# Latent attention in a two-layer block: maxima written negated, the rotation's last steps on GpSimd, and the former pair's sums and scaling ahead of the second head's last maxima

## The reference

```python
def mla_mixer(h, positions, w_in, q_g, kv_g, w_uq, w_ukv, w_out):
    """Non-causal multi-head latent attention with decoupled rotary key."""
    cq, ckv, kr = jnp.split(h @ w_in, [Q_LORA, Q_LORA + KV_LORA], axis=-1)
    q = (rms_norm_2(cq, q_g) @ w_uq).reshape(bsz, seq, C_HEADS, C_NOPE + C_ROPE)
    kv = (rms_norm_2(ckv, kv_g) @ w_ukv).reshape(bsz, seq, C_HEADS, C_NOPE + C_V)
    ...
    q_rope = apply_rope_2(q[..., C_NOPE:], cos, sin)
    k_rope = apply_rope_2(kr[:, :, None, :], cos, sin)
    ...
    def attend(qblk):
        s = jnp.einsum("bqhd,bkhd->bhqk", qblk, kf, preferred_element_type=jnp.float32) * scale
        pr = jax.nn.softmax(s, axis=-1)
        return jnp.einsum("bhqk,bkhd->bqhd", pr.astype(v.dtype), v)
    ...
    return o.reshape(bsz, seq, C_HEADS * C_V) @ w_out
```

## Time and profile before

| what | us |
|---|---|
| median of 3 runs | 1922.03 |
| the profiled execution, its own time | 1919.63 |
| its span, first to last instruction | 1917.8 |
| TensorE busy | 1860.2 (97%) |
| VectorE busy | 1153.8 (60%) |
| ScalarE busy | 736.8 (38%) |
| GpSimd busy | 166.2 (9%) |

### The profile page before, as it was taken

One profiled execution on the slowest core, in us unless ns is written; L12 is line 12 of the kernel. 1 busy time (PEld: TensorE's weight loads), 2 busy tenths in 40 slices (PEclk: granted clock), 3 DMA queues, 4 the chain that ended last, 5 costly groups with the idle time before them and its releaser, 6 DMA issues.

```text
span 1917.8 us, 24685 instructions
## 1 busy us (share of the span) xinstructions
PE 1860.2 (97%) x8914; PEld 1508.7 (79%) x8914; DVE 1153.8 (60%) x1645; ACT 736.8 (38%) x1074; POOL 166.2 (9%) x175
## 2 busy tenths in 40 slices
PE   7998999999999999999999999999999999999998
PEld 6786788888888877887788888888656688888887
DVE  7768644884674778777543434376788554334344
ACT  5355222542342444554432322334544342323231
POOL 0020000300000011010000000002366200000000
PEclk9998999999999999999999999999999999999999
DMA  5233003233333342311333333332110133333332
GB/s 211 88 121 99 1 3 122 64 99 99 98 89 99 99 121 77 94 60 45 93 99 97 92 96 98 99 98 78 56 34 23 45 88 99 99 98 92 95 99 88
DMA packets 47929, 165.68 MB, mean 86 GB/s; under 512 B 5217, under 2 KB 7265, under 8 KB 47713
## 3 DMA queue, kind: packets, MB, share of 16 engines
q1 hardware_dynamic: 46368, 161.27, 28.0%
q10 hardware_dynamic: 1472, 3.22, 0.5%
HBM read 162.38 MB, written 2.10 MB: 86 GB/s over the span
## 4 chain that ended last, share of the span: by engine, by line
PE 83%; DVE 10%; ACT 3%; issue 2%; POOL 1%; DMA 0%; DVEq 0%; ACTq 0%; POOLq 0%
PE ps L611 25%; PE ps L613 24%; PE ps L612 24%; PE ps L867 2%; PE ps L970 1%; DVE w_lo L2039 1%; POOL x L532 1%; PE ps L831 1%; DVE mla_mx L2634 1%; DVE tmp L2076 1%; ACT w_hi L1417 1%; PE ps L1216 1%; DVE qk_c L2753 0%; DVE mx L2556 0%; PE ps L800 0%
## 5 line engine op out<-in xcount | busy, mean ns | idle before, releaser
L1417 ACT ACTIVATE w_hi<-raw 128x1024 fp32r<-128x1024 f32 x281 | 297.7, 1060 | 792.1 <-PE ps L613 792.0
L611 PE MATMUL ps<-h_hi,w_hi 128*128 128x512 f32 (+1 forms) x1288 | 509.8, 396 | 10.9 <-DVE w_lo L2039 9.9
L612 PE MATMUL ps<-h_lo,w_hi 128*128 128x512 f32 (+1 forms) x1288 | 500.0, 388 | 0.0
L613 PE MATMUL ps<-h_hi,w_lo 128*128 128x512 f32 (+1 forms) x1288 | 499.9, 388 | 0.0
L2039 DVE TENSOR_TENSOR w_lo<-raw,w_hi 128x1024 fp32r<-128x1024 f32 x281 | 346.7, 1234 | 125.9 <-ACT w_hi L1417 124.4
L611 PEld LDWEIGHTS ps<-h_hi,w_hi 128*128 128x128 f32 x1288 | 243.3, 189 | 65.1 <-issue 13.0
L613 PEld LDWEIGHTS ps<-h_hi,w_lo 128*128 128x128 f32 x1288 | 243.0, 189 | 50.4
L612 PEld LDWEIGHTS ps<-h_lo,w_hi 128*128 128x128 f32 x1288 | 243.3, 189 | 49.9 <-issue 2.2
L611 PE MATMUL ps<-hid_hi,w_hi 128*128 128x512 f32 (+1 forms) x716 | 273.6, 382 | 1.7 <-DVE w_lo L2039 0.9
L613 PE MATMUL ps<-hid_hi,w_lo 128*128 128x512 f32 (+1 forms) x716 | 272.6, 381 | 0.0
L612 PE MATMUL ps<-hid_lo,w_hi 128*128 128x512 f32 (+1 forms) x716 | 272.6, 381 | 0.0
(11 more groups left out here) (404 smaller groups left out, 2524.2 us busy)
## 6 DMA issues: line engine op xcount, KB each, us to landing
raw<-in_panels SPq DMA_DIRECT2D x296, 512.0 KB, 3.6
x_in<-in_x SPq DMA_DIRECT2D x8, 256.0 KB, 5.7
x<-in_x ACTq DMA_DIRECT2D x1, 2048.0 KB, 8.4
out<-y SPq DMA_DIRECT2D x16, 128.0 KB, 1.8
first<-in_first SPq DMA_DIRECT2D x1, 1568.0 KB, 11.7
second<-in_second ACTq DMA_DIRECT2D x1, 512.0 KB, 3.5
small<-in_small ACTq DMA_DIRECT2D x1, 332.0 KB, 3.9
masks<-in_masks SPq DMA_DIRECT2D x1, 256.0 KB, 11.9
```

The costliest lines, as they stand in the source:

```text
L611: nc.tensor.matmul(out, a[0], b[0], start=start, stop=False)
L612: nc.tensor.matmul(out, a[0], b[1], start=False, stop=False)
L613: return nc.tensor.matmul(out, a[1], b[0], start=False, stop=stop)
L1417: nc.scalar.activation(w_high(panel, i), raw[:, panel % 4, :], ACT.Copy).then_inc(w_hi_ready, 1)
```

## The change

`mla_mx`, the instruction of line 2638 and its semaphore `negm_ready` are gone: the reduction writes the negated maximum straight into `mla_negm`, and `turn` waits for the fourth reduction. The bound by -1e20 is left out with it. `quad_finish` of the second, third and fourth group of four heads is issued by GpSimd, at the start of turns 2, 6 and 10, ahead of `pair_low` and `place_two`; the first group's stays on VectorE. In odd turns TensorE issues `totals(p - 1)` where `values(p, 0)` was, right behind scores 1, and `values(p, 0)` where `totals(p - 1)` was, behind scores 2 (in turn 1, where there are no totals, `values(0, 0)` moves too); VectorE does `shares` and `pair_result` ahead of largest 2 and 3 and `shift_of`, and no longer behind them.

```diff
+        def quad_finish(i):
+            pool.wait_ge(quad_taken, i + 1)
+            alone(nc.gpsimd.tensor_tensor(c_t[:, 1, :], c_t[:, 1, :], trig[:, 1, :], ALU.mult))
+            nc.gpsimd.tensor_tensor(c_t[:, 0, :], c_t[:, 0, :], c_t[:, 1, :], ALU.add).then_inc(quad_done, 1)
+            pool.wait_ge(quad_done, i + 1)
...
         for n in range(HEADS):
+            if n % 4 == 2 and n + 2 < HEADS:
+                quad_finish(n // 4 + 1)
             if n % 2 == 0 and n >= 4:
                 pair_low(n // 2 - 2)
...
         def turn(n):
-            pe.wait_ge(negm_ready, n + 1)
+            pe.wait_ge(mx_done, 4 * n + 4)
...
             scores(n, 1)
             if even and p + 1 < PAIRS:
                 project_nope(p + 1)
-            if not even:
-                values(p, 0)
+            if not even and p:
+                totals(p - 1)
             if more:
                 maxima(n + 1, range(2, 4))
             scores(n, 2)
...
             else:
-                if p:
-                    totals(p - 1)
+                values(p, 0)
                 values(p, 1)
                 scores(n, 3)
...
-                signal(V.tensor_reduce(mla_mx[:, n % 2, t:t + 1], ps[:, 2 + t % 2, :], AX.X, ALU.max), mx_done, wait=False)
-            if tiles.stop < NT:
-                return
-            dve.wait_ge(mx_done, 4 * n + 4)
-            signal(V.tensor_scalar(mla_negm[:, n % 2, :], mla_mx[:, n % 2, :], -1e20, -1.0, ALU.max, ALU.mult), negm_ready,
-                   wait=False)
+                signal(V.tensor_reduce(mla_negm[:, n % 2, t:t + 1], ps[:, 2 + t % 2, :], AX.X, ALU.max, negate=True), mx_done,
+                       wait=False)
...
             if even:
-                if n % 4 == 2 and n + 2 < HEADS:
-                    quad_finish(n // 4 + 1)
                 largest_of(n + 1, range(2, 4))
...
+                if p:
+                    shares(p - 1)
+                    pair_result(p - 1)
                 if more:
                     largest_of(n + 1, range(2, 4))
                     shift_of(n + 1)
-                if p:
-                    shares(p - 1)
-                    pair_result(p - 1)
```

More of the change, by code:

```diff
@@ L284, in build_in @@
         mla_total, mla_share = sq[:, 0, :], sq[:, 1, :]
-        mla_mx, mla_negm, mla_w = sb("mla_mx", [P, 2, 4], F32, c), sb("mla_negm", [P, 2, 4], F32, c), sb("mla_w", [P, 16], F32, c)
+        mla_negm, mla_w = sb("mla_negm", [P, 2, 4], F32, c), sb("mla_w", [P, 16], F32, c)
         warm = sb("warm", [P, 1], F32, c)
@@ L327, in build_in @@
         "block_s", "block_exp", "block_pv", "sum_taken", "token_ready", "token_turned", "token_high"))
-    mx_ready, mx_done, negm_ready, negm_turned, shift_ready, s_ready, exp_done, pv_done = (sem(n) for n in (
-        "mx_ready", "mx_done", "negm_ready", "negm_turned", "shift_ready", "s_ready", "exp_done", "pv_done"))
+    mx_ready, mx_done, negm_turned, shift_ready, s_ready, exp_done, pv_done = (sem(n) for n in (
+        "mx_ready", "mx_done", "negm_turned", "shift_ready", "s_ready", "exp_done", "pv_done"))
     token_out = sem("token_out")
```

## The result

The changed kernel takes 1932.97 us (median of five, 1926.26 to 1933.09) against 1921.99 us before, a ratio of 1.0052 with a 95% interval from 1.0040 to 1.0063. Run again on another occasion it took 1930.51 (six, 1925.38 to 1933.29) against 1921.21, ratio 1.0049 (1.0036 to 1.0061). The forecast was 1926.5 and the range ended at 1930: slower, as forecast, but by 11.0 and 9.3 us where 4.5 was forecast. The profiled execution was the fastest of its five, 1926.26 us with a span of 1924.5, where 1924.1 and 1922.3 were forecast. Of the 6.7 us between its span and that of the kernel before, 5.1 lie in the loop and 1.6 ahead of it, in parts that the change doesn't touch.

What follows compares the result with a forecast made beforehand. The prediction took TensorE, busy 97% of the span, as the bound; 13.2 us lost against 8.7 won gave 4.5 us more, 1926.5 us on the runs' median, with a range of 1921 to 1930.

Steps and rivals of the forecast that it cites:

- 7.5 us for line 2638: Attention loop: without line 2638, TensorE's transposes no longer wait for it, 7.5 us won.
- 1.2 for `project_nope`: Turns 6 and 10: earlier `quad_take` on VectorE ends a 0.60 us wait of `project_nope` in each, 1.2 us won.
- The wait at the sums: Odd turns 3 to 13: `totals`, moved earlier on TensorE, waits for VectorE's `k_lower`, 1.56 or 1.98 us each, 10.65 together.
- the release: At `totals`: a released wait needs 0.15 us to reach TensorE, six times, 0.9 us in all, bounds 0.4 and 1.6.
- both ends hang on the same transpose: End of `k_lower` and place of `totals` both follow the even turn's transpose, so the gap stays 1.56 and 1.98 us.
- Rivals 2 and 3: 2: VectorE sets pace, `k_lower` earlier, 0.8 us faster, chance 0.18; 3: sums' waits hardly exist, 7 us faster, chance 0.08.
- rival 4: Negated reductions take longer or GpSimd ends `quad_finish` over 2 us later: 3 to 6 us on top, about 1931, chance 0.04.
- The small terms: Attention loop, lost beside the sums' waits: releases 0.9, order of the turns 0.3, turn 13 0.5, turn 1 0.87 us.
- 0.87 for turn 1: Turn 1: maxima and values once done in the shadow ahead of scores 2 now come behind it, 0.87 us lost.
- turn 13's 2.22: Turn 13, 2.22 us longer: the wait for `k_lower`, plus 0.5 where VectorE's work, uncovered by `project_quad`, outlasts TensorE's.
- rival 1: Turns 3, 7, 11: the panel's low half is blocked by GpSimd too, 0.69 us more each, 1928.7 us, chance 0.10.
- The lost side of the sum: Attention loop: waits of `totals` 10.65 us plus 0.9, 0.3, 0.5 and 0.87, together 13.2 us lost.

Runs made afterwards that it cites:

- the two runs of single parts: Kernel before with one edit each: negated maxima alone, 1914.23 us, ratio 0.9967; `quad_finish` of later groups on GpSimd alone, 1922.2 against 1922.02 us, ratio 1.0002.
- the one at 1930.55: A further profiled execution of the unchanged copy of the changed kernel: 1930.55 us at a mean granted clock of 0.985.
- the filled kernel: Changed kernel, with TensorE repeating a matmul of the next maxima six times ahead of the sums of turns 3 to 13: 1925.88 us against 1930.51.

## Why the prediction was wrong

- *What the change wins.* Forecast 7.5 us for line 2638 and 1.2 for `project_nope`. Measured in the loop, in the old order: 147.32 - 139.69 = 7.63, and 139.69 - 138.26 = 1.43. Right.
- *The wait at the sums.* Forecast 1.56 and 1.98, plus 0.15 for the release: 1.71 and 2.13 behind the place where `totals` could have started. It started 1.76 and 2.20 to 2.25 behind it (1413.53 against 1411.54 + 0.23 in turn 5), in all six turns; the profile's idle time, 1.59 and 2.03 to 2.08, is shorter since a matmul's record outlasts the distance to the next. The reading that both ends hang on the same transpose, so that no saving elsewhere shortens it, held: from the transpose of turn 4 to the end of `k_lower` it is 5.35 us, as before. Rivals 2 and 3 are out, since the wait is there at full length; rival 4 too, by the two runs of single parts.
- *The small terms.* 0.87 for turn 1 was 0.85; turn 13's 2.22 was 2.13; the transposes of turns 13 and 14 wait 0.36 and 0.46, where 0.5 and 0.4 was forecast. The low half in turns 3, 7 and 11 still took 1.23, so rival 1 did not come about.
- *The lost side of the sum.* 13.2 forecast; 150.9 - 138.3 = 12.6 measured, clock left out. The order costs what the prediction said, against what the rest of the change alone would win. By itself, with line 2638 kept, it costs 5.9.
- *The step that failed* is the one that stood nowhere as a step. The earlier trace rows gave a granted clock of 1.00 for the loop, and the sum took it as given for the changed kernel too, although the change put waits of 1.6 to 2.1 us into a stretch in which no wait had been longer than 1.1 by the earlier trace rows. Each idle time was priced at its own length; some cost 1.5 us more. One such stretch is in the profiled execution, three in the one at 1930.55. With the waits filled the kernel is 4.7 us above the kernel before, which is the sum as forecast, and 4.6 us of the 9.3 are gone. In the timed executions the time follows the clock: at 0.988 the changed kernel takes 1925.4 and 1925.6, about 4 us above the kernel before at the same clock (1920.2 to 1923.0); at 0.984 it takes 1932.7 to 1933.3. The first median lies there, the second, 1930.51, at 0.985. So by estimate, of the 11 us between the first pair of medians some 4 to 5 are the sum as forecast and the rest the clock; of the 9.3 between the second, about half each.
- *The range and the chances.* There was no case for the clock, so the upper end lacked 3.0 us for the first median and 0.5 for the second. "Slower" had the highest chance, and the sign was right for the reason given.
- *What stays open.* The profiled executions of the changed kernel ran at 0.985 to 0.988. One at 0.984, as four of the first five, was not caught in a trace; that its further stretches lie behind the same waits is concluded from the filled kernel and from the execution at 1930.55, not seen. Stretches ahead of the loop, in parts that the change doesn't touch, differ from one execution to the next: in the thirteen traces the loop begins between 1362.3 and 1367.8 us. How much of the clock's share at 0.984 lies there is open. Why one wait of 1.59 us has such a stretch behind it and another of 2.08 has none, no run here settles.

## What to carry to other kernels

Before work is moved earlier in an in-order queue, write down for its new place what releases each of its waits, and follow that release back to the point where both engines last met; if nothing on that way gets shorter, the wait stays; here it could be read off to about 0.1 us. Then do the same for the next thing behind it: here the sums' bank and the chain to the next transpose bound at once, and undoing one alone brought little. And where TensorE is nearly always busy, a new wait of 1.6 to 2 us should be priced twice, with a case for a stretch at half clock behind it.

## What the runs showed of the hardware

TensorE's clock fell to its lower level around single waits of 1.6 to 2.1 us in a stretch where it was otherwise nearly always busy, though not at each of them: at one to three of six in the four traces of the changed kernel. It came back while TensorE worked on, with about 1.5 us lost. Waits of up to 1.1 us had no such stretch behind them in these loops. Six useless matmuls in each wait went with a clock of 1.00 throughout the traced loop and a kernel 4.6 us faster. The Trainium skill, page "TensorE: Matmul & The Clock Gate", section "HAM oscillation — how this bites in real kernels", tells of the clock falling behind waits of 3 to 5 us and in a short form warns of idle gaps beyond a length that none of the waits here reaches. The measurement decides: shorter ones are enough here, some of the time.

A four-column instruction of VectorE within SBUF, 0.17 us by itself, took 1.16 to 1.23 us when it began 0.06 to 0.15 us behind the start of a GpSimd addition, and 0.17 again when another order of the work moved that addition away. The waits view put that microsecond down to VectorE.
